# Modulation products of the first block on two column tiles of 64, with the diagonal picked from half as many columns

## The reference, cut to what matters

```python
mod = einsum('bd,de->be', silu(c), w_ada) + b_ada       # c: [1,1024], w_ada: [1024,6144]
sh1, sc1, g1, sh2, sc2, g2 = split(mod, 6)              # 1024 each
h = rms(x, norm1_g) * (1 + sc1) + sh1                   # x: [1,256,1024]
proj = h @ w_in                                         # -> MLA and differential attention
o_mla, o_diff = mla(...), diff_attn(...)
x = x + g1 * (concat(o_mla, o_diff) @ w_o)
h2 = rms(x, norm2_g) * (1 + sc2) + sh2
x = x + g2 * hmoe(h2, ...)
return second_block(x, ...)                             # two hybrid layers
```

## Time and profile before

| what | value |
|---|---|
| median of 3 runs | 2317.95 us (2314.77 to 2318.73) |
| profiled execution | 2320.38 us, span 2318.5 us |
| mean granted PE clock | 0.979 of full |
| busy share PE / PEld / DVE / ACT | 96% / 90% / 69% / 51% |
| chain that ended last, by engine | PE 90%, DVE 7%, ACT 2%, issue 1% |
| HBM read | 428.45 MB, 185 GB/s over the span |

### The profile page before, as it was taken

One profiled execution on the slowest core, in us unless ns is written; L12 is line 12 of the kernel. 1 busy time (PEld: TensorE's weight loads), 2 busy tenths in 40 slices (PEclk: granted clock), 3 DMA queues, 4 the chain that ended last, 5 costly groups with the idle time before them and its releaser, 6 DMA issues.

```text
span 2318.5 us, 37020 instructions
## 1 busy us (share of the span) xinstructions
PE 2231.9 (96%) x15858; PEld 2091.7 (90%) x15858; DVE 1609.3 (69%) x2014; ACT 1184.0 (51%) x1405; POOL 0.2 (0%) x4
## 2 busy tenths in 40 slices
PE   8989899999989999999998999899999999998997
PEld 7877788888889999999998999799999999998997
DVE  7986699999696668545566665596776445666763
ACT  3524477777554463534764444353554436745442
POOL 0000000000000000000000000000000000000000
PEclk9999899999999999999999999899999999999999
DMA  8453399999644544434334354344544444344552
GB/s 327 164 181 115 127 345 372 371 372 370 254 165 150 198 146 164 164 128 163 112 126 164 131 179 170 121 171 157 188 163 163 162 146 151 106 162 146 183 187 86
DMA packets 64307, 431.92 MB, mean 186 GB/s; under 512 B 7792, under 2 KB 11152, under 8 KB 13712
## 3 DMA queue, kind: packets, MB, share of 16 engines
q1 hardware_dynamic: 64144, 429.56, 51.3%
HBM read 428.45 MB, written 1.08 MB: 185 GB/s over the span
## 4 chain that ended last, share of the span: by engine, by line
PE 90%; DVE 7%; ACT 2%; issue 1%; DMA 0%; SPq 0%; DVEq 0%; ACTq 0%
PE banks L1819 62%; PE banks L1837 10%; PE quad L1837 5%; PE single L1554 1%; DVE area_y L2291 1%; PE quad L1554 1%; PE quad L552 1%; PE single L565 1%; PE quad L516 1%; PE quad L452 1%; DVE slot_rounded L998 1%; PE quad L555 1%; PE quad L500 1%; PE quad L540 1%; DVE slot_rounded L2328 0%
## 5 line engine op out<-in xcount | busy, mean ns | idle before, releaser
L1819 PE MATMUL banks<-spare_rounded,slot_rounded 128*128 128x272 f32 (+1 forms) x2176 | 624.1, 287 | 0.0
L1819 PE MATMUL banks<-spare_rounded,area_y_rounded 128*128 128x272 f32 (+1 forms) x1504 | 438.6, 292 | 15.3 <-DVE hn_rounded L987 13.3
L1819 PE MATMUL banks<-area_x_rounded,slot_rounded 128*128 128x272 f32 (+1 forms) x1568 | 447.1, 285 | 0.0
L1819 PE MATMUL banks<-hn_rounded,area_y_rounded 128*128 128x272 f32 (+1 forms) x1504 | 431.8, 287 | 0.0
L1819 PEld LDWEIGHTS banks<-spare_rounded,slot_rounded 128*128 128x128 f32 x2176 | 412.6, 190 | 0.0
L998 DVE TENSOR_TENSOR slot_rounded<-slot,area_y_rounded 128x2048 fp32r<-128x2048 f32 x118 | 269.6, 2289 | 161.2 <-ACT area_y_rounded L650 161.2
L1819 PEld LDWEIGHTS banks<-spare_rounded,area_y_rounded 128*128 128x128 f32 x1504 | 285.8, 190 | 17.7 <-DVE hn_rounded L987 14.2
L1819 PEld LDWEIGHTS banks<-area_x_rounded,slot_rounded 128*128 128x128 f32 x1568 | 296.9, 189 | 0.0
L1819 PEld LDWEIGHTS banks<-hn_rounded,area_y_rounded 128*128 128x128 f32 x1504 | 285.4, 190 | 0.1
L650 ACT ACTIVATE area_y_rounded<-slot 128x2048 fp32r<-128x2048 f32 x118 | 223.7, 1906 | 32.8 <-PE banks L1819 32.8
L998 DVE TENSOR_TENSOR slot_rounded<-slot,area_x_rounded 128x2048 fp32r<-128x2048 f32 x52 | 119.0, 2292 | 93.1 <-ACT area_x_rounded L650 93.0
(11 more groups left out here) (543 smaller groups left out, 5193.7 us busy)
## 6 DMA issues: line engine op xcount, KB each, us to landing
slot<-in_units_second SPq DMA_DIRECT2D x236, 1024.0 KB, 4.8
slot<-in_units_moe SPq DMA_DIRECT2D x100, 1024.0 KB, 5.2
slot<-in_units_first SPq DMA_DIRECT2D x32, 1024.0 KB, 4.9
spare<-in_units_moe SPq DMA_DIRECT2D x20, 1024.0 KB, 5.3
spare<-in_units_first SPq DMA_DIRECT2D x6, 1024.0 KB, 4.8
slot<-in_units_second SPq DMA_DIRECT2D x8, 768.0 KB, 4.2
merged<-acs_rows SPq DMA_DIRECT2D x4, 544.0 KB, 5.2
slot<-in_units_first SPq DMA_DIRECT2D x2, 576.0 KB, 3.7
```

The lines of the kernel that those rows point to most:

```text
L1819: ins = nc.tensor.matmul(out, weights[w], x[a], start=start and i == 0, stop=stop and i == 2, **kw)
```

## The change

Each of the eight matmuls of a unit becomes two. Both have a stationary side of 64 columns of the same broadcast instead of 128. The first writes output partitions 0 to 63, the second 64 to 127, which are two column tiles of the array. The first takes as moving side the columns 0 to 63 and 128 to 191 of the unit's block, the second 64 to 127 and 192 to 255: of each square of 128 x 128 only the half in which the diagonal of these partitions lies. A unit so fills 128 columns of PSUM instead of 256, and a pair 256 instead of 512. `diagonal` works on four pieces of 128 x 64; its mask is `m.folded`, the two halves of the identity added, made once by a new reduction on DVE before the root of x. The products `diagonal_early` and `diagonal_late` shrink to [128, 4, 64], and the reductions read half as much. The new lines move the line numbers: L1554 becomes L1557, L1819 becomes L1823, L2314 becomes L2318, L2337 and L2338 become L2343 and L2344.

```diff
+ADA_TILE = 64
@@ ada_rows
         for k in range(KT):
-            ins = nc.tensor.matmul(m.ada_part(u), m.silu_c[:, k:k + 1].to_broadcast([128, 128]), w[:, k * UNIT_COLS:(k + 1) * UNIT_COLS],
-                                   start=(k == 0), stop=(k == KT - 1))
+            unit = w[:, k * UNIT_COLS:(k + 1) * UNIT_COLS].rearrange("p (a b) -> p a b", a=2)
+            for j in range(0, 128, ADA_TILE):
+                ins = nc.tensor.matmul(m.ada_part(u)[j:j + ADA_TILE, :].rearrange("p (a b) -> p a b", a=2),
+                                       m.silu_c[:, k:k + 1].to_broadcast([128, ADA_TILE]), unit[:, :, j:j + ADA_TILE],
+                                       start=(k == 0), stop=(k == KT - 1), skip_group_check=True)
         tick(ins, s.gemm_first)
@@ first_vector
     def diagonal(bank, out, signal):
-        tick(tt(out, bank.rearrange("p (a b) -> p a b", b=128), m.ident.unsqueeze(1).to_broadcast([128, 4, 128]), ALU.mult), signal)
+        tick(tt(out, bank[:, 0:4 * ADA_TILE].rearrange("p (a b) -> p a b", b=ADA_TILE), m.folded.unsqueeze(1).to_broadcast([128, 4, ADA_TILE]), ALU.mult), signal)
         settle()
...
+    v.wait_ge(m.loaded_early.sem, 16)
+    tick(red(m.folded, m.ident.rearrange("p (a b) -> p b a", b=ADA_TILE), AX_X, ALU.add), s.dve1_step)
     v.wait_ge(s.x_root.sem, 1)
@@ memory
-        m.diagonal_early, m.diagonal_late = (work[:, at:at + 512].rearrange("p (a b) -> p a b", b=128) for at in (0, 2048))
+        m.diagonal_early, m.diagonal_late = (work[:, at:at + 4 * ADA_TILE].rearrange("p (a b) -> p a b", b=ADA_TILE) for at in (0, 2048))
+        m.folded = work[:, 2560 - ADA_TILE:2560]
...
-        m.ada_part = lambda u: (m.ada_bank(u % 4)[:, 256 * (u // 4):256 * (u // 4) + 256] if u < 8 else m.single[:, 256 * (u % 2):256 * (u % 2) + 256])
+        m.ada_part = lambda u: (m.ada_bank(u % 4) if u < 8 else m.single)[:, 2 * ADA_TILE * (u // 4 if u < 8 else u % 2):][:, 0:2 * ADA_TILE]
```

## The result

The changed kernel takes 2307.45 us (median of 7 runs, 2305.0 to 2308.82); the kernel before, run beside it, 2318.02 us (7 runs, 2314.77 to 2323.25). The ratio is 0.9947 [0.9937, 0.9957]: 10.6 us faster. That is inside the range of 2293 to 2309, 8.0 us above the forecast of 2299.5, and just above 2306.5, the sum's own worst case. The profiled execution took 2305.62 us with a span of 2303.5 and a mean granted clock of 0.976, against 0.979 before.

A forecast was written before the change was run, and what follows sets the result against it. PE was taken to carry the chain after the first block, DVE much of that block. 6.7 + 0 + 1.1 + 4.75 + 4.9 + 3.6 - 2.5 = 18.5 us off 2320.4, less 2.4 to the median: 2299.5 us, range 2293 to 2309.

The forecast's parts named there:

- the sum's own worst case: Whole program: all bounds taken against the sum, 11.6 us gained, 2306.5 us.
- A unit on PE: Each modulation unit's products: 1.9 us instead of 3.45, including 0.15 us for the change of tiling.
- Both rivals of this step: Unit's products: tiles don't work together, 3.6 us a unit, 2317, chance 0.07; weight loads don't hide, 4.1 us, 2324.5, 0.04.
- The early pairs: First four pairs of units, to 48.23 us: DVE is the bound in every pair and ends at 41.6, gaining 6.7 us.
- 48 to 118 us: Stretch after the early pairs: both engines move together, gain 0, down to -1.5 if cold PE uses up the slack.
- the wait of 0.57: DVE's wait at the two units at 117.90: saved, with 0.54 of DVE's own work, together 1.1 us.
- The loop and its end: Attention loop: first half gains 4.75 and 4.9 us, second half 0; units at the end gain 3.6 us.
- The clock takes some back: PE stops near 32 us and in loop rounds bring half clock: 2.5 us lost, bounds 0 and 6.
- the clock eats it: Rival, attention loop: slow rounds make PE the bound, the middle's 10.7 us mostly goes, about 8 us gained, 2310; chance 0.09.
- the wait of 5.92 us: DVE's wait at 183.02 in the loop: falls to 1.5, gaining 4.4 us (2.8 to 5.9), plus 0.54 for the reading.

The follow-up runs named there:

- Early alone: Kernel before with only the eight early units on two column tiles, later units and their readings unchanged: 2311.1 us, 0.9970, 6.9 us off.
- the product made twice: Changed kernel with the mask's product done twice in each of 12 readings: 2309.55 us, 0.9964.
- two stops filled: Changed kernel plus unread products of ones: seven per turn of the attention loop, twelve before the third pair of keys' transposes: 2300.2 us, 0.9919.
- a stop filled in the kernel before: Kernel before plus twelve unread products of ones ahead of the seventh head's probabilities: 2315.11 us, 0.9985.
- its third: Third profile of the changed kernel, unaltered, from the twelfth run: median 2307.08 us, 0.9953.
- A slower order of the same products: Changed kernel with its loops exchanged, all eight products of the lower column tile, then all eight of the upper: 2308.22 us, 0.9957.

## Why the prediction was right, and where it was short

*A unit on PE.* Right, 1.75 us against 1.9. The 0.15 for changes of the tiling do not show inside a row of units. Both rivals of this step fell by the spacing of 0.109 us: the tiles work together, and the loads add nothing. The Trainium skill (TensorE: Matmul & The Clock Gate, Part 3: Packing small matmuls — row/col tiling, The mechanism) has loads overlap only where row groups differ; here both tiles use all 128 rows and the load of 0.137 us still costs nothing. The measurement decides.

*The early pairs.* Right: between the first and the fourth pair the forecast gained 6.1 - 1.0 = 5.1 us, and the traces show 5.4. Early alone is worth 6.9 us in all. DVE was the bound: it never waits at a reading, and the product made twice moves each pair by its 0.45 us.

*48 to 118 us.* Right, 0: DVE's lead is 5.9 us near 80 and 6.5 at 124.85, where the wait of 0.57 went. The chain now runs through PE, which worked off its stop at half clock, and through the transfer at 74.29. One reading of mine here was wrong. Against the clock's rival I held that PE had stood some 2.5 of 3 us ahead of 82.8 at full clock. The window right behind, kernel before:

```profile
82.90:86.30 3.40, 3.40 (x17) 3.40 (x18) 3.37 (x7) 1.49 (x4) 0.00 (x0) 0.52 0.47 195
```

Half clock followed that stop too, so it spoke for the rival.

*The loop and its end.* The mechanism was right where the clock is full: with two stops filled the waits are 0.42 us or less at the readings of the loop but one (0.45), and the last two readings are 8.89 us apart instead of 11.81: 2.9 us less, where two units and the reading were to give 3.4. In the changed kernel itself they are 10.50 apart, only 1.3 us less. With a stop filled in the kernel before and two in the changed one, the change is worth 2315.11 - 2300.2 = 14.9 us; my terms without the clock add up to 21.0. Of the 6.1 between, 2.9 are the wait that I took at 5.92 and that is 1.53 at full clock; the rest holds the filling's own price and is not separated.

*The step that failed, by its size: "The clock takes some back".* I took 2.5 us with a bound of 6. Filling the stops at the keys and in the loop gives 6.9 us, net of what the filling costs, so the term was at least 4.4 us too small, over half of the 8.0 us, and its bound too tight. Two things were missing. I listed PE's stops near 32 us and in the rounds, and not the one for the keys at 115 to 120, which is 3.55 to 4.27 us; in two traces of three 10.2 us from it on are at half clock. And I priced a slow stretch by the transposes on the chain of the second half, and held the first half covered by slack; but at half clock a unit is 3.63 us again, and DVE waits for it (2.85 us at 167.71). The rival *the clock eats it* was right in kind: its 2310 is 2.6 us off, the forecast 8.0. That the time lies in the range at all is due to this rival, for which the range was drawn to 2309; the sum's own bounds, all taken against it, missed it.

*The second size: the wait of 5.92 us.* Another execution has the wait at 3.18 us, 2.7 less, and is some 5 us faster (2315.23 against 2320.38). The profiled execution was slow partly for this wait; I counted the wait as a gain, and then took off once more the 2.4 us by which that execution lies above the median. Without the clock's term my sum stands at 2297.0, and the kernel with two stops filled at 2300.2: 3.2 us are left. The 2.4 taken twice and the filling's own price (its lead falls from 16.4 to 15.2 us between the reading of 183.02 and the next) both go that way; their shares were not measured. That 4.4 and 3.2 make nearly the 8.0 is arithmetic and shows nothing more.

*What stays open.* Why the same kernel meets a slow stretch at the keys in two executions of three is not shown. Nor is why the lead of the first trace falls by some 3 us behind 300 us (16.4 to 13.5), or how much of the gain is DVE's shorter reading.

## What to carry to other kernels

Taking work off TensorE without shortening what it waits for made stops here, and they were paid in clock: list every stop behind the removed work, not only those in the loop, and try cheap products there; here they turned 10.6 us into about 18 (2300.2 us against 2318.29 of the kernel before). Such products cost time where they stand ahead of work that is ready. Before a wait is priced from one trace, look at the granted clock over it, and at a second execution. Full-fp32 products of which only a diagonal is wanted can go on two column tiles with half of the columns each: 1.75 us a unit here instead of 3.45.

## What the runs showed that I had not expected

- Column tiles issued one after the other still overlap where the tile changes: 2.8 us a unit against 1.75 issued in turn and 3.5 with none.
- Loads of 64 columns (0.137 us each, 160 of them within 8.6 us) are under way two or three at a time, and pairs of passes still follow each other at 0.109 us.
- Two column tiles with full width cost what one product of 128 columns does: 0.219 us against 0.216 a block and pass.
- One kernel's execution is not one clock: 17.0 us at half clock in the loop of the changed kernel's first trace, 30.6 in its third, in executions only 0.7 us apart (2305.62 and 2306.31).
- A slower order of the same products left PE's clock at 0.98 in the loop, against 0.84 to 0.91, and the program took the same time.
